# Scaling of the attention probabilities in the second mixer, moved from VectorE to GpSimd

## Reference, cut to what matters

```
def block(qblk):
    s = jnp.einsum('bhgqd,bhkd->bhgqk', qblk, k_all).astype(jnp.float32) * scale
    pr = jax.nn.softmax(s, axis=-1).astype(v_all.dtype)
    return jnp.einsum('bhgqk,bhkd->bhgqd', pr, v_all)
```

## Time and profile before

| what | value |
|---|---|
| median of 3 runs | 1571.29 us (1570.74 to 1572.24) |
| the profiled execution, its own time | 1571.23 us |
| its span, first to last instruction | 1569.5 us |
| PE (TensorE matmul) busy | 1554.4 us, 99% |
| DVE (VectorE) busy | 1057.9 us, 67% |
| ACT (ScalarE) busy | 551.3 us, 35% |
| POOL (GpSimd) busy | 24.3 us, 2% |

### The profile page before, as it was taken

How to read it: one execution, slowest core, us unless ns; L and a number is a source line. 1 busy time by engine, 2 the same in 40 slices (tenths; PEclk the granted TensorE clock), 3 DMA queues, 4 the chain that set the end, 5 groups by cost and what they waited for, 6 DMA issues and landing times.

```text
span 1569.5 us, 21740 instructions
## 1 busy us (share of the span) xinstructions
PE 1554.4 (99%) x8578; PEld 1324.2 (84%) x8578; DVE 1057.9 (67%) x1576; ACT 551.3 (35%) x841; POOL 24.3 (2%) x66
## 2 busy tenths in 40 slices
PE   8999999999999999999999999999999999999998
PEld 5898988778899888888888888988888888888887
DVE  4999999888848883677526437857867543444346
ACT  5423225684722221222211226533326332222233
POOL 0000000220000000000000000000000000000000
PEclk9999999999999999999999999999999999999999
DMA  9622132124135453455233231330022233233232
GB/s 323 207 70 81 55 108 72 63 83 146 41 123 199 160 188 121 148 182 207 93 110 105 62 100 54 125 121 28 1 67 68 87 101 109 79 107 107 81 101 87
DMA packets 132746, 171.54 MB, mean 109 GB/s; under 512 B 16114, under 2 KB 88498, under 8 KB 132666
## 3 DMA queue, kind: packets, MB, share of 16 engines
q1 hardware_dynamic: 131770, 168.25, 33.5%
q0 software_dynamic: 640, 2.10, 0.3%
q10 hardware_dynamic: 256, 0.08, 0.0%
HBM read 166.17 MB, written 2.15 MB: 107 GB/s over the span
## 4 chain that ended last, share of the span: by engine, by line
PE 95%; ACT 2%; DMA 1%; DVE 1%; SPq 0%; issue 0%; POOL 0%; DVEq 0%
PE acc L737 51%; PE acc L786 26%; PE acc L763 5%; PE acc L1213 2%; PE acc L1148 2%; PE acc L1009 2%; PE acc L877 1%; DMA ada<-in_ada_w 1%; PE acc L1161 1%; PE acc L777 1%; PE acc L915 1%; PE acc L1041 1%; ACT probs L1499 1%; PE acc L1118 0%; PE acc L696 0%; PE acc L713 0%
## 5 line engine op out<-in xcount | busy, mean ns | idle before, releaser
L737 PE MATMUL acc<-h_hi,w_hi 128*128 128x512 f32 (+1 forms) x1424 | 494.5, 351 | 0.0
L737 PE MATMUL acc<-h_lo,w_hi 128*128 128x512 f32 (+1 forms) x1424 | 492.5, 350 | 0.0
L737 PE MATMUL acc<-h_hi,w_lo 128*128 128x512 f32 (+1 forms) x1424 | 492.2, 349 | 0.0
L1712 DVE TENSOR_TENSOR w_lo<-raw,w_hi 128x1024 fp32r<-128x1024 f32 x183 | 218.2, 1220 | 135.3 <-ACT w_hi L1233 135.2
L737 PEld LDWEIGHTS acc<-h_hi,w_lo 128*128 128x128 f32 x1424 | 267.1, 189 | 35.1
L737 PEld LDWEIGHTS acc<-h_hi,w_hi 128*128 128x128 f32 x1424 | 267.3, 189 | 34.5
L737 PEld LDWEIGHTS acc<-h_lo,w_hi 128*128 128x128 f32 x1424 | 267.3, 189 | 33.8
L1233 ACT ACTIVATE w_hi<-raw 128x1024 fp32r<-128x1024 f32 x183 | 186.6, 1053 | 214.9 <-PE acc L786 151.7
L786 PE MATMUL acc<-w_hi,hid_hi 128*128 128x512 f32 x434 | 169.5, 391 | 0.0
L786 PE MATMUL acc<-w_hi,hid_lo 128*128 128x512 f32 x434 | 168.9, 389 | 0.0
L786 PE MATMUL acc<-w_lo,hid_hi 128*128 128x512 f32 x434 | 168.8, 389 | 0.0
(11 more groups left out here) (289 smaller groups left out, 2039.4 us busy)
## 6 DMA issues: line engine op xcount, KB each, us to landing
ada_w<-in_ada_w SPq DMA_DIRECT2D x96, 512.0 KB, 5.5
raw<-in_ffn_w_in SPq DMA_DIRECT2D x88, 512.0 KB, 3.6
raw<-in_ffn_w_out SPq DMA_DIRECT2D x44, 512.0 KB, 4.2
raw<-in_even_w_in SPq DMA_DIRECT2D x24, 512.0 KB, 4.5
ada<-in_ada_w SPq DMA_DIRECT2D x8, 1024.0 KB, 11.9
raw<-in_odd_w_in SPq DMA_DIRECT2D x12, 512.0 KB, 3.5
raw<-in_even_w_out SPq DMA_DIRECT2D x8, 512.0 KB, 5.6
raw<-in_odd_w_out SPq DMA_DIRECT2D x8, 512.0 KB, 4.2
```

The lines of the kernel that those rows point to most:

```text
L737: last = nc.tensor.matmul(acc[:, s, m, t0:t1], w[:, slot, kk, c], x_[:, k, t0:t1], start=(k == 0 and q == 0), stop=(k == KD - 1 and q == 2))
L1712: return nc.vector.tensor_tensor(out_, in0, in1, op)
```

## The change

VectorE keeps the reciprocal and signals a new semaphore, `inverse_ready`. GpSimd gets a loop of 24 steps behind its last DMA: it waits for `inverse_ready` and scales `ptile` in place by the same operation, on the same buffer, signalling the same `pn_ready`.

```diff
--- before.py
+++ after.py
@@ -2487,10 +2487,7 @@
                     nc.vector.tensor_copy(pT[:, (n - 1) % 2, :], acc[:, 1, 0, 0:T]).then_inc(sem("pT_ready"), 1)
                 if n < N_Q * NL:
                     dve.wait_ge(sem("score_exp"), n + 1)
-                    sd.done(nc.vector.reciprocal(arow[:, n, 3:4], arow[:, n, 2:3]))
-                    sd.wait()
-                    nc.vector.tensor_scalar(ptile[:, n % 2, :], ptile[:, n % 2, :], arow[:, n, 3:4], None, ALU.mult
-                                            ).then_inc(sem("pn_ready"), 1)
+                    nc.vector.reciprocal(arow[:, n, 3:4], arow[:, n, 2:3]).then_inc(sem("inverse_ready"), 1)
                     if n % NL == 2 and n > NL:
                         head_low(n // NL - 1)
             dve.wait_ge(sem("pool_high"), 1)
@@ -2536,6 +2533,11 @@
                 x_ = inb[:, 2 + 2 * v:4 + 2 * v, :] if v < 3 else kT[:, :, 0:LAT]
                 for odd in range(2):
                     nc.gpsimd.dma_start(swapped[1 - odd::2, v % 2], x_[odd::2]).then_inc(sem(f"swapped_in{v}"), 16)
+
+            for n in range(N_Q * NL):
+                pool.wait_ge(sem("inverse_ready"), n + 1)
+                nc.gpsimd.tensor_scalar(ptile[:, n % 2, :], ptile[:, n % 2, :], arow[:, n, 3:4], None, ALU.mult
+                                        ).then_inc(sem("pn_ready"), 1)
 
 
 _INS = ("x", "c", "ctx", "c_ctx", "ada_w", "ada_b", "mix_pre_g", "mix_post_g", "ffn_pre_g", "ffn_post_g", "ffn_w_in",
```

## The result

The changed kernel took 1593.41 us (median of 4 runs, 1592.62 to 1593.76) against 1571.15 for the kernel before (now the median of four): 1.0141 times as long, 95% interval 1.0129 to 1.0153, or 22.3 us more. The forecast was 1571.5 in a range up to 1581.0, so it was wrong.

A forecast was written before the change was run, and what follows sets the result against it. TensorE was taken to bound the attention at 3.31 us a step. The profiled 1571.23 us, gain 0 from VectorE's relief, plus 0.25 of loss from GpSimd's path gave 1571.5, in a range of 1570.7 to 1581.0.

The forecast's parts named there:

- what bounds the kernel: In the attention, TensorE is busy for all 50 us of the window and holds the chain, 3.31 us a step.
- the worth of the relief: Removing 24 scalings of 0.62 us, 14.9 us, from VectorE was counted as a gain of 0.
- the ring: Attention loop of transposes, copy, reciprocal and GpSimd's multiply: period 1.99 + s, above TensorE's 3.31 us beyond s = 1.32.
- the room: From the end of VectorE's reciprocal to the load of the transposes: 1.32 us in steps 2 to 22.
- D: Total loss, (s - 0.94) + 21 x (s - 1.32), each bracket at least 0; forecast 0.25 us at s = 1.19.
- Added, the multiply: GpSimd's scaling of 768 elements in each step: 1.03 us, midway between 0.78 and 1.27; six masks, 1.75, above.
- the first rival: GpSimd's multiply in the loop becomes the bound, slower: 1574.0 us at 1.27, 1584.6 at 1.75; chance over 0.2%: 0.26.
- The rival of blocking: GpSimd's multiply must wait for VectorE's maximum behind the reciprocal, 0.95 us: loss 18.4, time 1589.6; chance 0.05.
- The rival of a gain: VectorE's relief shortens a TensorE wait, at the start: perhaps 0 to 1 us; chance of over 0.2% faster 0.03.

The follow-up runs named there:

- with the mask: The changed kernel with GpSimd's multiply replaced by the first mixer's masking operation over 768 columns, keeping everything, normalisation left out: 1571.1 us, ratio 0.9998.

## Why the prediction was wrong

*Right: what bounds the kernel, and the worth of the relief.* VectorE's scaling was off the chain; taking it away brings nothing that three runs could measure.

*Right: the ring and its limit.* It was forecast as a period of 1.99 + s with s the whole path through GpSimd, and 1.16 us as the limit of the multiply. Measured, the period is the multiply plus 2.07 to 2.09 in every run that had the ring: 4.29 with 2.20, 4.55 with 2 x 1.24, 4.21 with 2.13, 3.54 with 1.47, 3.56 with 1.47. The limit is 3.31 - 2.08 = 1.23. The three whole-width operations below it (0.83, 0.83, 0.94) cost nothing, and 1.22 only what the five tighter steps give. That the room is 1.32 in all of steps 2 to 22 also held: the kernel before left less in nine of them, down to 0.95, but with the mask, where VectorE has no part of the scaling, each leaves 1.32, and step 1 leaves 0.95. Put with 2.20 into the prediction's own formula, s = 2.35 and D = 1.41 + 21 x 1.03 = 23.0, against 22.3 measured. The formula's 1.99 was 0.05 too long: in the changed kernel the rest of the ring is 4.29 - 2.35 = 1.94, which makes it 22.0.

*Wrong: the price of the multiply.* The step that failed is "Added, the multiply": 1.03 us, from a floor of 0.78 and the mask's 1.27, with six masks, 1.75, as the ceiling. It was 2.20, above all three. The argument was that the mask works out a comparison per element where the multiply has one operation, and so is dearer. The runs show the opposite: mask 0.83 us, copy 0.83, product of two tensors 1.47, product with a scalar 2.20. The same multiplication costs 1.47 or 2.20 by the form of the instruction, and the mask with its comparison costs no more than a copy: among these, the amount of arithmetic doesn't tell the price. The floor of 0.78 held. The mask itself was misread too, 1.27 for 0.83, because its fixed part is 0.19 and not the memset's 0.1. The ceiling was no ceiling, as it too belonged to another operation. What happened is the first rival, GpSimd as the bound, at a price above any that it was worked out for (1.75 us, 1584.6). Its "against it" was that a simple multiply would have to be slower per element than the mask, and that is what it was, 2.51 ns against 0.83.

*The rule weighed against the rows.* The Trainium skill, page "GPSIMD Engine Reference", section 8 (Key points), says that VectorE is structurally about twice as fast for elementwise work. Measured, it is 2204 / 620 = 3.6 times as fast for this form. The rule had the right sign and still gave only 2.1 us of loss. The Trainium skill, page "GPSIMD Engine Reference", section 3.1, gives 4497 ns for an addition of two tensors of 2048 elements; that is 2.2 ns an element, and an estimate of 1.7 us for the product of two tensors here. 1.47 was measured, with the second tensor a repeated column.

*The rival of blocking* gave a time of 1589.6, nearer than the forecast, but that is luck, as its reason is wrong. Maximum and copy don't hold GpSimd up: 2202 to 2207 ns in all 24 steps. That agrees with the rule that the prediction took from the Trainium skill, page "SBUF — State Buffer", section "Who interferes with whom", on VectorE instructions with at most one SBUF input, outside the 2-port modes. The two engines do hold each other up where VectorE's scaling runs beside GpSimd, and the change leaves no such place. The Trainium skill, page "SBUF — State Buffer", the same section, states that for a VectorE instruction in a 2-port mode, which it says `tensor_scalar` can enter, the one that comes second is blocked for the whole instruction of the first. In which mode the scaling runs no trace shows. Beside GpSimd's multiply that does not hold: VectorE's scaling came second and ended after 1.24 us, while the multiply took 2.20. Beside the memset it can't be excluded, as 0.84 us of waiting and 0.40 for 768 elements make 1.24 too (620 and 420 ns for 768 and 384 columns are 0.52 ns an element).

*The rival of a gain.* No run with VectorE relieved was faster beyond its interval, as the prediction expected.

## What to carry to other kernels

Before moving an operation to an idle engine, find the ring in which its result runs back to its own start, and read off the trace the limit at which the ring overtakes the bound. Then price the operation by a row of the same form on the same engine; if there is none, the range has to hold a price of several times the nearest row, and the move needs a test of that one instruction. If the moved work must stay slow, taking one instruction out of the ring's order (here the reciprocal ahead of the copy) or another form (two tensors in place of a scalar) gives back most of the loss: 16 or 17 of the 22 us here. No version that was tried is faster than the kernel before.

## What the runs showed that was not expected

- GpSimd on 128 x 768 fp32: copy 0.829 us, mask 0.826, product of two tensors 1.466, product with a scalar per partition 2.204, with a constant 2.128. The scalar form with a scalar per partition costs 2.51 ns an element over 0.28 us.
- VectorE's scaling of 128 x 768 takes 1.24 to 1.25 us instead of 0.62 when a GpSimd instruction has begun 0.07 to 0.11 us earlier, be it a multiply of 2.20 us or a memset of 0.95. Begun 0.06 us before GpSimd's multiply, VectorE's part lengthens that one by 0.23 us (384 columns, 0.42 long) or an estimated 0.30 (512 columns, 0.49 long). Both are 0.13 less than what VectorE still had to run when GpSimd began, 0.36 and 0.43. That would fit a GpSimd that waits for VectorE's end with 0.13 us of its own start-up meanwhile, but no run tests it.
